# Two transformer layers in split fp32 on one core: order of subtractions, of ff1's first halves and of x's low part

## The reference, cut to what matters

```python
def hybrid_layer(x, positions, norm_mix, w_in, b_gate, ..., w_branch, w_out, norm_ff, w_ff1, w_ff2):
    h = rms_norm(x, norm_mix)
    proj = h @ w_in
    ...
    ys = jnp.stack([y_nsa, y_sb, y_gla, y_fox], axis=2)
    branch = jnp.einsum('bsnc,ncd->bsnd', ys, w_branch)
    gates = jax.nn.sigmoid((gate_logits + b_gate).astype(jnp.float32)).astype(x.dtype)
    mixed = jnp.sum(gates.reshape(B, S, N_BRANCH, D_MODEL) * branch, axis=2)
    x = x + mixed @ w_out
    h2 = rms_norm(x, norm_ff)
    return x + jnp.square(jax.nn.relu(h2 @ w_ff1)) @ w_ff2

def second_block(x, ...):
    for l in range(2):
        x = hybrid_layer(x, ...)
    return rms_norm(x, norm_final)
```

## Time and profile before

| what | value |
|---|---|
| median of 3 runs | 1735.07 us (1734.69 to 1735.87) |
| the profiled execution's own time | 1736.49 us |
| its span, first to last instruction | 1734.7 us |
| TensorE busy | 1665.3 us, 96% |
| VectorE busy | 907.5 us, 52% |
| ScalarE busy | 731.6 us, 42% |
| GpSimd busy | 136.4 us, 8% |
| mean granted TensorE clock | 0.991 of full |
| mean read rate | 242 GB/s |

### The profile page before, as it was taken

How to read it: one execution, slowest core, us unless ns; L and a number is a source line. 1 busy time by engine, 2 the same in 40 slices (tenths; PEclk the granted TensorE clock), 3 DMA queues, 4 the chain that set the end, 5 groups by cost and what they waited for, 6 DMA issues and landing times.

```text
span 1734.7 us, 23489 instructions
## 1 busy us (share of the span) xinstructions
PE 1665.3 (96%) x9607; PEld 1247.0 (72%) x9607; DVE 907.5 (52%) x1532; ACT 731.6 (42%) x1101; POOL 136.4 (8%) x133
## 2 busy tenths in 40 slices
PE   7999998988998979999999999999999999999998
PEld 6987434443444369888788788888978878878886
DVE  6584211111121065755588777536665557977743
ACT  4564111110111145655546355324655554545532
POOL 0000000000000001323200000000323210000000
PEclk9999999999999999999999999999999999999999
DMA  7447999999999946434463445535543445435552
GB/s 288 171 182 297 400 426 427 428 428 429 428 428 425 422 182 244 170 115 159 156 223 150 151 190 194 203 146 220 193 160 146 158 165 187 182 146 194 194 203 85
DMA packets 38080, 420.49 MB, mean 242 GB/s; under 512 B 3968, under 2 KB 5600, under 8 KB 10976
## 3 DMA queue, kind: packets, MB, share of 16 engines
q1 hardware_dynamic: 37984, 419.12, 61.2%
HBM read 417.24 MB, written 1.87 MB: 242 GB/s over the span
## 4 chain that ended last, share of the span: by engine, by line
PE 83%; DMA 8%; DVE 6%; issue 2%; ACT 1%; POOL 0%; SPq 0%; POOLq 0%; DVEq 0%; ACTq 0%
PE bank L1281 10%; DMA work_mem<-in_w 7%; PE bank L1944 7%; PE bank L1500 5%; PE bank L1501 5%; PE bank L1506 5%; PE bank L1476 4%; PE bank L1474 4%; PE bank L1475 4%; PE bank L1948 4%; PE bank L1306 3%; PE bank L1438 3%; PE bank L1445 3%; PE bank L1439 3%; DVE w_lo L3042 1%
## 5 line engine op out<-in xcount | busy, mean ns | idle before, releaser
L2228 ACT ACTIVATE w_hi_early<-wring 128x2048 fp32r<-128x2048 f32 x84 | 160.9, 1916 | 221.2 <-PE bank L1506 120.6
L3042 DVE TENSOR_TENSOR w_lo<-wring,w_hi 128x2048 fp32r<-128x2048 f32 x84 | 191.9, 2291 | 118.7 <-ACT w_hi L2228 118.7
L2228 ACT ACTIVATE w_hi<-wring 128x2048 fp32r<-128x2048 f32 x84 | 161.0, 1917 | 201.7 <-PE bank L1475 89.9
L3042 DVE TENSOR_TENSOR w_lo<-wring,w_hi_early 128x2048 fp32r<-128x2048 f32 x84 | 203.6, 2428 | 42.5 <-ACT w_hi_early L2228 42.2
L1281 PE MATMUL bank<-wring,gates_mem 128*64 128x512 f32 x720 | 164.8, 604 | 9.7 <-DMA wring<-in_w 9.7
L1500 PE MATMUL bank<-w_hi_early,mixed 128*128 128x512 f32 x384 | 151.7, 395 | 0.0
L2944 DVE TENSOR_TENSOR gates_mem<-bank,gates_mem 128x512 f32<-128x512 f32 x32 | 22.1, 692 | 244.8 <-ACT gates_mem L2176 136.2
L1501 PE MATMUL bank<-w_hi_early,mixed 128*128 128x512 f32 x384 | 149.7, 390 | 0.0
L1944 PE MATMUL bank<-mixed,w_hi 128*128 128x512 f32 x512 | 129.5, 393 | 1.5 <-DVE mixed L3050 1.4
L1281 PEld LDWEIGHTS bank<-wring,gates_mem 128*64 128x64 f32 x720 | 54.6, 139 | 103.8 <-issue 103.7
L1944 PEld LDWEIGHTS bank<-mixed,w_hi 128*128 128x128 f32 x512 | 91.7, 189 | 19.3 <-DVE mixed L3050 3.2
(11 more groups left out here) (532 smaller groups left out, 3144.3 us busy)
## 6 DMA issues: line engine op xcount, KB each, us to landing
wring<-in_w SPq DMA_DIRECT2D x157, 2048.0 KB, 8.6
work_mem<-in_w SPq DMA_DIRECT2D x33, 2048.0 KB, 17.1
gates_mem<-rel_skew SPq DMA_DIRECT2D x16, 512.0 KB, 9.2
work_mem<-in_w SPq DMA_DIRECT2D x2, 1024.0 KB, 13.1
cst<-in_const SPq DMA_DIRECT2D x1, 1224.0 KB, 15.8
prm<-in_prm SPq DMA_DIRECT2D x3, 381.0 KB, 8.6
x_mem<-in_x SPq DMA_DIRECT2D x2, 512.0 KB, 4.4
low_high<-in_w SPq DMA_DIRECT2D x1, 1024.0 KB, 10.9
```

Source lines behind the costliest of these rows:

```text
L2228: act.activation(hi, w, ACT.Copy).then_inc(hi_ready, 1)
L3042: dve.tensor_tensor(lo, w, hi, ALU.subtract).then_inc(lo_ready, 1)
```

## The change

It has four parts, all in both layers.

1. Start of a layer, TensorE: `split_first` makes all 16 high-by-high products first, waiting for ScalarE's high parts of h alone, then the low weights for tile 0, then the 16 products with h's low part, then the low weights for tile 1. The next three halves are taken with `high_half` and the wait for the low weights stands behind tile 0's high passes.
2. Start of a layer, VectorE: the subtraction of half 0 comes before `low_x`, that of half 1 before the scaling of x (first layer), that of half 2 behind it.
3. Branches, VectorE: the subtraction of RINGED+0 moves ahead of the wait for GpSimd's rstd8 and of the two multiplications that give `y_gla`; that of LATE+8 moves behind `gated_two(12)`.
4. ff1, TensorE: its first two halves are cut by feature tile. Tiles 0 to 3 of half 0 come before the transposes into `h2[2:4]`, tiles 0 to 3 of half 1 behind these, and then tiles 4 to 7 of both. In every half the high passes of both output tiles now come before the low ones. The bank table is dealt out to match.

```diff
@@ plan_layer @@
-                        ("mixed_t", 2), ("out", 2), ("h2", 4), ("ff1", 32), ("ff2", 4)):
+                        ("mixed_t", 2), ("out", 2), ("h2", 2), ("ff1", 2), ("h2", 2), ("ff1", 30), ("ff2", 4)):
@@ TensorE, split_first @@
-                    out, w = psum[j.bank][:, 0:S], hi[:, :, t * P:(t + 1) * P]
+                    for k in range(KT):
+                        if t == 0 and k % 2 == 0:
+                            pe.wait_ge(h2_hi_ready, len(pre["ht"]) + 24 * l + k // 2 + 1)
+                        pe.matmul(psum[j.bank][:, 0:S], hi[:, k, t * P:(t + 1) * P], h_hi[:, k, :], start=(k == 0), stop=False)
+                half_ready(0)
+
+                def low_pass(t):
+
+                    for k in range(KT):
+                        mm = pe.matmul(psum[jobs[t].bank][:, 0:S], lo[:, k, t * P:(t + 1) * P], h_hi[:, k, :], start=False,
+                                       stop=(t == 1 and k == KT - 1))
+                        if t == 1 and k == 0:
+                            mm.then_inc(half_used, 1)
+                    return mm
+
+                low_pass(0)
+                for t, j in enumerate(jobs):
                     for k in range(KT):
                         if t == 0 and k % 2 == 0:
                             turned = layer["ht"][k // 2]
                             pe.wait_ge(bank_read[turned.bank], turned.count(l))
-                        pe.matmul(out, w[:, k, :], h_hi[:, k, :], start=(k == 0), stop=False)
-                        pe.matmul(out, w[:, k, :], h_lo[:, k, :], start=False, stop=False)
-                half_ready(0)
...
+                        mm = pe.matmul(psum[j.bank][:, 0:S], hi[:, k, t * P:(t + 1) * P], h_lo[:, k, :], start=False,
+                                       stop=(t == 0 and k == KT - 1))
+                    if t == 0:
+                        mm.then_inc(bank_full[j.bank], 1)
+                low_pass(1).then_inc(bank_full[jobs[1].bank], 1)
@@ TensorE, the halves behind it @@
-            split_a(layer["nsa_k"][2], half_ready(1), 0, h_parts, True)
+            split_a(layer["nsa_k"][2], high_half(1), 0, h_parts, True, low=1)
...
-            split_a(layer["nsa_q"][0], half_ready(2), 0, h_parts, True)
+            split_a(layer["nsa_q"][0], high_half(2), 0, h_parts, True, low=2)
...
-            split_a(layer["nsa_q"][1], half_ready(3), 0, h_parts, True)
+            split_a(layer["nsa_q"][1], high_half(3), 0, h_parts, True, low=3)
@@ TensorE, ahead of the transposes into h2[2:4] @@
+            def ff1_high(n, ks):
+
+                hi, lo = half_ready(LATE + 12 + n)
+                for t, j in enumerate(layer["ff1"][2 * n:2 * n + 2]):
+                    if ks[0] == 0:
+                        free(j, l)
+                    out, cols = psum[j.bank][:, :].rearrange("p (a s) -> p a s", a=2), slice(t * P, (t + 1) * P)
+                    for k in ks:
+                        mm = pe.matmul(out, hi[:, k, cols], mixed_both[:, :, k, :], start=(k == 0), stop=False)
+                if ks[-1] == KT - 1:
+                    mm.then_inc(half_used, 1)
+
+            def ff1_low(n, ks):
+
+                hi, lo = weight_half(LATE + 12 + n)[2:]
+                for t, j in enumerate(layer["ff1"][2 * n:2 * n + 2]):
+                    for k in ks:
+                        mm = pe.matmul(psum[j.bank][:, 0:S], lo[:, k, t * P:(t + 1) * P], h2_hi[:, k, :], start=False,
+                                       stop=(k == KT - 1))
+                    if ks[-1] == KT - 1:
+                        mm.then_inc(bank_full[j.bank], 1)
+
+            in_sbuf(layer["h2"][0:2], l)
+            ff1_high(0, range(4))
+            ff1_low(0, range(4))
@@ TensorE, behind them (ff1(n) for n in range(16) goes) @@
+            ff1_high(1, range(4))
+            ff1_low(1, range(4))
+            in_sbuf(layer["h2"][2:4], l)
+            for n in range(2):
+                ff1_high(n, range(4, KT))
+                ff1_low(n, range(4, KT))
+            for n in range(2, 16):
+                ff1_high(n, range(KT))
+                ff1_low(n, range(KT))
@@ VectorE, start of a layer @@
+            split_lo(0)
             low_x(layer["ht"], at2["norm_mix"], h_lo, 0)
-            split_lo(0)
+            next_lo(0)
             if l == 0:
...
-            for h in range(2):
-                next_lo(h)
+            next_lo(1)
@@ VectorE, branches @@
             y_low(1)
+            split_lo(RINGED + 0)
             dve.wait_ge(rstd8_ready, l + 3)
             then(dve.tensor_tensor(heads8(o_g), heads8(o_g), by_head(rstd8), ALU.mult))
             dve.tensor_tensor(o_g, o_g, sig_gg, ALU.mult).then_inc(y_gla, 1)
-            split_lo(RINGED + 0)
...
             split_lo(RINGED + 5)
+            gated_two(12)
             split_lo(LATE + 8)
-            gated_two(12)
             mixed_low(0)
```

25 lines of the change are left out of this document (removed).

## The result

| | before | after |
|---|---|---|
| first comparison, median | 1735.44 us (4 runs, 1734.69 to 1735.87) | 1723.22 us (4 runs, 1721.77 to 1724.9) |
| second comparison, median | 1736.71 us (9 runs, 1735.24 to 1737.17) | 1723.12 us (5 runs, 1721.46 to 1724.66) |
| ratio, first comparison | | 0.993, 95% interval 0.9913 to 0.9948 |
| ratio, second comparison | | 0.9918, 95% interval 0.9905 to 0.9932 |
| the profiled execution's own time | 1736.49 us | 1724.9 us |

What follows compares the result with a forecast made beforehand. TensorE, busy 96% of the span, was taken as the bound; 1.9 + 0.5 + 4.0 + 1.7 + 3.5 + 0.5 = 12.1 us, giving 1723.7 us, range 1719.5 to 1728.5; faster by over 0.2% had chance 0.94.

Steps and rivals of the forecast that it cites:

- A: Start of the two layers: the half behind `split_first` starts earlier, gaining 1.9 us in the first layer and 0.5 in the second.
- Rival 3: Layer start: loads set it, so the gain there and part of the branches' is swallowed; 1726 to 1728 us, chance 0.06.
- B: Branches: moving the subtractions of RINGED+0 and LATE+8 gains 2.0 us a layer, 4.0 in all; subtraction and GpSimd's power exclude each other.
- rival 1: Branches: no lock between GpSimd and VectorE, VectorE 1.5 us ahead; 0.6 a layer more, 1722.5 us, chance 0.08.
- the few tenths of waiting left at `turn_mixed(0)`: Branches: the mix's first half is ready at about 965.5, TensorE there at 965.2, so it still waits a few tenths.
- The 0.3 for the subtraction ahead of `mixed_low(0)`: Branches, ahead of `turn_mixed(1)`: the moved 2.24 us subtraction meets 2 us of idle time; 0.3 lost, bounds 0 and 2.24.
- The wait at L1476's place: Branches: TensorE's wait for VectorE at 937.52, priced at 0.45 + 0.16 = 0.61 us, was to go.
- The clock: Behind `turn_mixed(0)`, first layer: with the standstill cut to a few tenths, no clock drop; 1.7 us, bounds 0 and 1.7.
- rival 2: Clock: the drop stays or another standstill brings one, each costing 1.7 us; 1725.4 for one, 1727.1 for two; chance 0.10.
- C: ff1's start, last transposes to third half: less waiting for h2's parts; 1.75 us a layer, 3.5 for both, bounds 1.75 and 3.7.
- Switches: ff1's halves: high passes side by side mean fewer changes of matmul shape; 0.25 us a layer, 0.5 in all, bounds 0 and 1.
- Rivals 4 and 5: 4: VectorE decides in branches and at ff1, only 4 us gained, 1731, chance 0.04; 5: late `y_gla` makes it slower, 0.02.

## Why the prediction was right, and where it was not

**The time.** 1723.7 was forecast, 1723.22 and 1723.12 were measured, inside the range and on the side that was given 0.94. Part of this is two errors that cancel. The layers gave more than the sum of 12.1, and the median of before, from three runs, was 1.4 to 2.1 lower than the medians of 26, 9 and 7 runs (1736.49, 1736.71, 1737.15). That the forecast time came within 0.6 us is luck to that extent; the gain, 11.4 on the median's footing, was 12.2 and 13.6.

**A, 1.9 and 0.5.** Measured 1.87 and 0.42 with this part alone; the 2.08 of the profile after has 0.2 from the lower clock in it. The steps were seen as described: VectorE's idle time holds the first layer's subtraction, and `low_x` is pushed in the second. Rival 3, loads that set the layer's start, is out: with this part alone nothing was given back up to gla's transposes.

**B, 2.0 a layer. This is the step that failed.** "The subtraction stands beside the power now, and one waits for the other": it was not so. The rows had shown two things, that the power waits for a VectorE instruction of two SBUF operands, and that a subtraction is held off by a GpSimd instruction (2.79 instead of 2.29). The second was seen behind an instruction of 128x768, and I applied it to the power. The run with the subtraction first showed the wait of the power for the VectorE instruction in flight (3.65 us), and next to it VectorE instructions that wait for nothing. So rival 1 was right in what follows, VectorE 1.5 us ahead behind the pair; its name, no lock at all, is not, and its price of 0.6 a layer was low. The Trainium skill, page "SBUF — State Buffer", section "Who interferes with whom", that the prediction cites says that a VectorE instruction with two SBUF inputs contends with a GpSimd instruction that reads SBUF, by an exclusive lock in which the order of issue decides who blocks. For VectorE's instruction ahead of the power the trace agrees (2.59 and 3.65), and for GpSimd's of 128x768 ahead of VectorE's too (3.36); for the power ahead of VectorE's it does not, since only its wait and not the 1.5 us of its own run was exclusive.

The other terms: the few tenths of waiting left at `turn_mixed(0)`, 0.3 in the sum, were 0. The 0.3 for the subtraction ahead of `mixed_low(0)` was 0 and 0.08. The wait at L1476's place costs 0.75 in the first layer (305.47 against 304.72 with RINGED+0 alone) and not 0.61, because the matmuls behind the standstill, the second above all, come 0.14 later than at the usual pace. Together it is 2.9 us a layer instead of 2.0.

**The clock, 1.7.** In the profile of before it was that: 9.87 against 8.22. But rival 2's ground was right too: at 2.0 us of standstill 3 of 8 layers have it, so a typical execution of before loses 2 × 3/8 × 1.6 = 1.2 us. The change removes it at this place, in all its profiles, and one drop came elsewhere, at a price of 0.8.

**C, 3.5.** Measured 3.74, and 3.81 alone, a little above the upper bound of 3.7. The cover held: no wait for `mixed` above what TensorE shows as 0. **Switches, 0.5:** 0.52, and the run that undoes the grouping gives it back.

**Rivals 4 and 5.** The change did what it says. `y_gla` did come later, by 0.6 us (936.08 − 930.25 = 5.83 behind the start of `y_low(1)`, where it was 935.27 − 930.02 = 5.25), but TensorE wanted it only at 938.95; even with the subtraction put first TensorE lost no more than 0.56 us.

With the sizes of undisturbed profiles the sum is 2.3 + 5.7 + 1.2 + 3.7 + 0.5 = 13.4 us, beside measured 12.2 and 13.6.

## What to carry to other kernels

On a kernel that one engine fills to 96%, list that engine's waits inside the stage, ask for each what stands ahead of the releasing instruction in its queue, and move whatever is not yet wanted behind it: such moves were worth 12 to 14 us here without removing an instruction. When one engine is seen to wait for another, note which of the two waited, behind which instruction and of what size, and do not carry it over to another pair. When a stretch is compared between profiles, look at the granted clock ahead of it too: slower work in front can make it look 0.2 to 0.6 us shorter. Where the reference time comes from few runs, its own uncertainty (1.4 us and more here) can be as large as a term of the sum.

## What the runs showed of the hardware

- GpSimd's power of 128 × 8 waits for the end of the VectorE instruction that is in flight at its start (2.59 us in all beside one of 1.23, 3.65 beside one of 2.29) and then takes 1.5 us, in which VectorE's instructions with two SBUF inputs run at their plain 1.22 and 2.29 us. Behind GpSimd instructions of 128 × 768 the same subtraction of 2.29 us took 2.78 to 3.85, each time ending 2.15 us behind GpSimd's end.
- A standstill of TensorE of 2.0 us was followed by the lower clock (1.2 GHz) in 3 of 8 layers, one of 4.5 us in 2 of 2, one of 1.15 us in 0 of 2, none in 0 of 14; the price was 1.6 us, once 2.6.
- At a layer's start, where ScalarE and VectorE follow TensorE, the lower clock once lengthened the second layer's 32 transposes by 1.4 us (5.17 against 3.77) and shortened the stretch behind them by 0.6 (6.62 against 7.19).
- A wait of 0.45 us in TensorE's row at a matmul of 512 columns cost 0.75 us of time.
- Working ff1's halves as one block of 512-column matmuls and one of 256 saves 0.02 us a half against two of each.
